# Retention stage: the decode tokens' value rows spread before the outputs, state pairs read between projections, four rows spread at once in the last head

## The chip, the cores and the metric

The kernel runs on one core of one Trainium2 chip. The metric is the device time of one execution in microseconds (us); three executions of the kernel before gave 3306.15, 3307.99 and 3312.09, median 3307.99. The profile is one further execution.

## The reference

The program is one inference step of a 4-layer decoder for 512 prompt tokens and 8 decode tokens that share weights. Layers 0 and 3 use retention as their mixer, layer 1 pooling, layer 2 sparse attention; each is followed by a SwiGLU block and layer norms. The change touches retention only. For a head with keys of 256 and values of 512 the decode part is, for each of the 8 decode tokens b:

```
S_new[b] = gamma * S_old[b] + k[b] (256) outer v[b] (512)      # written back as an output
o[b]     = q[b] @ S_new[b]                                     # 512 values, then normalised and gated
```

For the prompt part, o = (q k^T * decay) v over chunks of 128, and the final state is S = sum over tokens of decayed k outer v. Both parts go through the same weights: y = (silu(g) * normalised o) @ w_out.

## The kernel before

All products with weights are done as three float32r matmuls (high*high, high*low, low*high), in "units" of 128 output columns over 520 tokens (two halves of 260). For a retention layer a head has units 0 to 11 (q, k, v, gate) and 12 to 19 (output projection); unit(i, k) on TensorE waits until the accumulator of two units before is evacuated. ScalarE makes the high part of a weight tile (L445), VectorE the low part (L451): `step(k)` on both engines makes the parts of the unit that is two places on, and it waits for the matmuls of unit k. Accumulators lie in PSUM banks 0 to 3, everything else in banks 4 to 7.

Every engine has its own hand-written order of work; semaphores tie them. Names that the change and the prediction use:

- `outputs(t)` (TensorE, L524 to L526): prompt outputs of chunk t, (t+1) groups of three matmuls of 512 columns. `stats(i, t)` and `centre(i, t)` (VectorE, L1268 to L1277) normalise them, with `rstd` on GpSimd (L614, L616) between.
- `spread_v(i, b)` (TensorE, L1933 and L1934): copies the value row of decode token b to all 128 partitions of bank 7 with two matmuls. It waits until the state of token b-1 is updated (`s_new`), since all rows use one bank.
- `new_state(i, b)` (VectorE, L1300): two instructions that add k[b] times the spread row to the state of token b in place. It waits for `vb` (the spread row) and `st_sc` (state loaded by GpSimd's queue at L608 and scaled by ScalarE at L849).
- `read_states(i, g)` (TensorE, L1943): eight matmuls that read the states of tokens 2g and 2g+1; it waits for their updates. `state_out` and `refill` (GpSimd, L620 and L608) write a state out and load a later one into its buffer; there are four buffers for eight tokens.
- `final_state(d)` (TensorE, L524 to L526), `turn_outputs` (TensorE, L1813 and, for the decode rows, L1914), `gate` and `gate_lo` (VectorE, L1285 and L1291), `gain(n)` (VectorE, L1258).

Heads follow one another: `tail(n)` does the decode work of tokens 4 to 7 of head i-1 between the units of head i. The last head (i = RH - 1 = 3) has no next head, so it does that work by itself before its output projection.

Of the kernel before, what the change touches and what calls it, by code (L numbers as in the profile page):

```python
# [25 lines left out]
SEQ = 512  # L26
NB = 8
T = SEQ + NB
HALF = T // 2
QT = SEQ // P  # L30
# [3 lines left out]
RH, RK, RV = 4, 256, 512  # L34
# [203 lines left out]

VT_BANK, AT_BANK, O_BANK, SF_BANK = [6, 7, 4, 5, 4], [4, 5, 6, 7], [5, 4, 5, 4, 6], [5, 4]
OT_BANK = [5, 4, 5, 4, 7]  # L240


def trunk(nc, A, O):

    with ExitStack() as ctx:
        marks = Marks(nc, ctx)
        S = marks.sem
        V, C, G, M = nc.vector, nc.scalar, nc.gpsimd, nc.tensor
# [22 lines left out]
        ps = ctx.enter_context(nc.psum_tensor("ps", [P, 8, 512], F32))  # L271
# [315 lines left out]
        def _(pool):  # L587
# [4 lines left out]
            def ret(stage):  # L592
                j = int(stage[3:]) // 3
                s_in = A["state_ret"][j].rearrange("b h (d p) e -> h b p d e", p=P)
                s_out = O[3][j].rearrange("b h (d p) e -> h b p d e", p=P)

                def head(ap, i, b=None):
                    return ap[i] if b is None else ap[i, b]

                def head_constants(i):  # L600
                    pool.dma_start(mask, head(A["decay"], i)).then_inc(S["head_in"], 16)
                    pool.dma_start(hc(i, 0, 8), head(A["head_col"], i)).then_inc(S["head_in"], 16)
                    gains = A["ret_norm_g"][j].rearrange("(h c p) -> h p c", p=P, c=VC)
                    with nc.allow_non_contiguous_dma("columns of gains"):
                        pool.dma_start(hc(i, 8, 12), head(gains, i)).then_inc(S["head_in"], 16)

                def state_in(i, b):
                    pool.dma_start(st[:, b % 4], head(s_in, i, b)).then_inc(S[f"st_in{b % 4}"], 16)  # L608

                def rstd(at, t):  # L610

                    n = P if t < QT else 36
                    pool.wait_ge(*at("o_ag", t + 1))
                    G.tensor_scalar(ve[0:n, t:t + 1], mv[0:n, t, 1:2], EPS, None, ALU.add).then_inc(S["rs_e"], 1)  # L614
                    pool.wait_ge(*at("rs_e", t + 1))
                    G.tensor_tensor(rs[0:n, t:t + 1], ve[0:n, t:t + 1], mhalf[0:n, :], ALU.pow).then_inc(S["rs_p"], 1)  # L616

                def state_out(at, i, b):
                    pool.wait_ge(*at("s_new", 2 * b + 2))
                    pool.dma_start(head(s_out, i, b), st[:, b % 4]).then_inc(S[f"st_out{b % 4}"], 16)  # L620

                head_constants(0)
                for b in range(4):
                    state_in(0, b)
                for i in range(RH):
                    at = marks.here(stage, i)

                    def refill(b):

                        pool.wait_ge(*at(f"st_out{b % 4}", 16 * (1 + b // 4)))  # L630
                        pool.wait_ge(*at("so_mm", b // 2 + 1))
                        if b < 4:
                            state_in(i, b + 4)
                        elif i < RH - 1:
                            state_in(i + 1, b - 4)

                    rstd(at, 0)
                    rstd(at, 1)
                    state_out(at, i, 0)
                    state_out(at, i, 1)  # L640
                    rstd(at, 2)
                    rstd(at, 3)
                    state_out(at, i, 2)
                    state_out(at, i, 3)
                    refill(0)
                    refill(1)
                    pool.wait_ge(*at("sf_cp", 2))
                    pool.dma_start(head(O[2][j, 0].rearrange("h (d p) e -> h p d e", p=P), i), sf).then_inc(S["sf_out"], 16)
                    if i < RH - 1:
                        pool.wait_ge(*at("att_m", 4))  # L650
                        head_constants(i + 1)
                    refill(2)
                    refill(3)
                    for b in range(4, 8):
                        state_out(at, i, b)
                    rstd(at, 4)
                    for b in range(4, 8):
                        refill(b)
# [501 lines left out]
        def _(dve):  # L1160
# [35 lines left out]
            def ret(stage):  # L1196
# [3 lines left out]
                def before_gates(i):  # L1200
# [55 lines left out]
                    def gain(n):  # L1256
                        dve.wait_ge(*at("sil_g", n + 1))
                        V.tensor_scalar(sg[:, n], sg[:, n], hc(i, 8 + n, 9 + n), None, ALU.mult  # L1258
                                        ).then_inc(S["sg_n"], 1)
# [34 lines left out]
                    def new_state(i, b):  # L1294

                        at = marks.here(stage, i)
                        dve.wait_ge(*at("vb", b + 1))
                        dve.wait_ge(*at("st_sc", b + 1))
                        for d in range(KC):
                            V.scalar_tensor_tensor(st[:, b % 4, d], ps[:, 7, :], k_f[:, d, SEQ + b:SEQ + b + 1],  # L1300
                                                   st[:, b % 4, d], ALU.mult, ALU.add).then_inc(S["s_new"], 1)

                    def step(k):
# [68 lines left out]
                    gain(0)  # L1372
                    step(9)
                    gain(1)
                    stats(i, 0)
                    stats(i, 1)
                    new_state(i, 0)
                    centre(i, 0)
                    centre(i, 1)
                    step(10)  # L1380
                    gain(2)
                    new_state(i, 1)
                    stats(i, 2)
                    stats(i, 3)
                    centre(i, 2)
                    centre(i, 3)
                    new_state(i, 2)
                    step(11)
                    gain(3)
                    new_state(i, 3)  # L1390
                    gate(i, 0)
                    gate(i, 1)
                    gate_lo(i, 0)
# [417 lines left out]
        def _(pe):  # L1811
# [14 lines left out]
            def ret(stage):  # L1826
# [31 lines left out]
                for i in range(RH):  # L1858
# [67 lines left out]
                    def spread_v(i, b):  # L1926

                        at = marks.here(stage, i)
                        pe.wait_ge(*at("v_lo", 5))
                        if b:  # L1930
                            pe.wait_ge(*at("s_new", 2 * b))
                        one = ident_r[0:NB, b:b + 1].to_broadcast([NB, P])
                        M.matmul(ps[:, 7, :], one, v_h[0:NB, QT, :], start=True, stop=False)  # L1933
                        M.matmul(ps[:, 7, :], one, v_l[0:NB, QT, :], start=False, stop=True).then_inc(S["vb"], 1)  # L1934

                    def read_states(i, g):

# [10 lines left out]
                    def tail(n):  # L1948

                        if not i:  # L1950
                            return
                        h = i - 1
                        if n == 0:
                            turn_outputs(h, 2, ("gate_m", 1))
                            turn_outputs(h, 3, ("gate_m", 2))
                            spread_v(h, 4)
                        elif n == 1:
                            read_states(h, 1)
                            spread_v(h, 5)
                        elif n == 2:  # L1960
                            read_states(h, 2)
                            spread_v(h, 6)
                        elif n == 3:
                            spread_v(h, 7)
                        elif n == 4:
                            read_states(h, 3)
# [28 lines left out]
                    values(3, ("att_m", 2))  # L1995
                    values(4, ("v_lo", 3))
                    unit(i, 9)
                    outputs(0, ("v_lo", 4))
                    outputs(1, ("v_lo", 5))
                    spread_v(i, 0)  # L2000
                    unit(i, 10)
                    spread_v(i, 1)
                    outputs(2, ("o_n", 1))
                    outputs(3, ("o_n", 2))
                    spread_v(i, 2)
                    unit(i, 11)
                    spread_v(i, 3)
                    final_state(0, ("o_n", 3))
                    final_state(1, ("o_n", 4))
                    read_states(i, 0)  # L2010
                    turn_outputs(i, 0, ("sf_cp", 1))
                    turn_outputs(i, 1, ("sf_cp", 2))
                    if i == RH - 1:
                        read_states(i, 1)
                        turn_outputs(i, 2, ("gate_m", 1))
                        turn_outputs(i, 3, ("gate_m", 2))
                        for b in range(4, 8):
                            spread_v(i, b)
                            if b % 2:
                                read_states(i, b // 2)  # L2020
                        turn_outputs(i, 4, ("s_new", 2 * NB))
                        project(i)

# [269 lines left out]
            for stage, n, units in STAGES:  # L2293
# [25 lines left out]
                elif kind == "end":  # L2319
                    at = marks.here(stage)  # L2320
# [65 lines left out]
```

## Time and profile before

| what | value |
|---|---|
| median of three executions | 3307.99 us |
| profiled execution, its own time | 3312.6 us |
| its span, first to last instruction | 3310.9 us |
| mean granted TensorE clock | 0.951 |
| TensorE matmul busy | 3082.7 us (93%) |
| VectorE busy | 1567.0 us (47%) |
| ScalarE busy | 1016.1 us (31%) |
| GpSimd busy | 223.9 us (7%) |

The two retention layers lie in the first fifth of the span and behind its 2330th us. A head repeats every 128.72 us (second spread of a head at 101.83, 230.54, 359.26 us). The granted clock is given as a share: 1.00 is 2.4 GHz and 0.50 is 1.2 GHz.

### The profile page before, as it was taken

To read this page: it belongs to the slowest core of one execution; us is meant where nothing else is said; L and a number is where in the kernel's file an instruction comes from. 1 tells how busy PE (TensorE), PEld (TensorE's weight loads), DVE (VectorE), ACT (ScalarE), POOL (GpSimd) and SP (SyncE) were. 2 spreads that over 40 slices of the span, in tenths; PEclk is the share of its full clock that TensorE was granted. 3 is DMA by queue.
4 is the path that set the end of the run, shared out by engine and by line. 5 is a ranking of instruction groups with operands and counts; after the bars stand their busy time and mean duration, and the time that the engine had idled before them with its cause. 6 is when DMAs were issued, how large, how long until landed. Compare 5 with 4: busy or idle time off the path is not lost.

```text
span 3310.9 us, 54894 instructions
## 1 busy us (share of the span) xinstructions
PE 3082.7 (93%) x23315; PEld 2901.3 (88%) x23315; DVE 1567.0 (47%) x2418; ACT 1016.1 (31%) x1428; POOL 223.9 (7%) x350
## 2 busy tenths in 40 slices
PE   8999997999976999988787899999999999799997
PEld 7898895999975999987677799999889989599996
DVE  4555555333357333358765453234555555533234
ACT  3333332322233222232333142222523333332223
POOL 0111111000000000010001100000021011100000
PEclk9999997999987999999888899999899999799998
DMA  6345333232311332321122323233244433333230
GB/s 146 131 132 159 128 115 124 81 111 71 103 50 54 92 99 83 102 65 44 52 58 71 121 71 103 82 89 96 87 149 125 148 131 115 109 89 108 76 101 35
DMA packets 491331, 323.11 MB, mean 98 GB/s; under 512 B 29179, under 2 KB 467707, under 8 KB 491130
## 3 DMA queue, kind: packets, MB, share of 16 engines
q1 hardware_dynamic: 464338, 230.14, 24.4%
q0 software_dynamic: 26800, 90.18, 8.0%
q8 instruction: 148, 2.42, 0.3%
q14 instruction: 45, 0.37, 0.0%
HBM read 275.90 MB, written 44.82 MB: 97 GB/s over the span
## 4 chain that ended last, share of the span: by engine, by line
PE 75%; issue 14%; DVE 8%; ACT 2%; POOL 0%; DMA 0%; another core or an unknown queue 0%; POOLq 0%; SPq 0%; ACTq 0%; DVEq 0%
PE ps L474 59%; PE ps L1813 2%; PE ps L524 2%; PE ps L1943 2%; PE ps L526 2%; PE ps L525 2%; PE ps L505 1%; PE ps L1933 1%; DVE wf L1533 1%; DVE tiny L1531 1%; DVE wf L1778 1%; PE ps L2276 1%; DVE x_l L1165 1%; PE ps L2288 1%; DVE w_l L451 1%
## 5 line engine op out<-in xcount | busy, mean ns | idle before, releaser
L474 PE MATMUL ps<-x_h,w_h 128*128 128x260 f32 x4576 | 941.6, 287 | 10.4 <-DVE w_l L451 8.2
L474 PE MATMUL ps<-x_h,w_l 128*128 128x260 f32 x4576 | 927.9, 285 | 0.0
L474 PE MATMUL ps<-x_l,w_h 128*128 128x260 f32 x4576 | 926.9, 284 | 0.0
L451 DVE TENSOR_TENSOR w_l<-w_raw,w_h 128x1024 fp32r<-128x1024 f32 (+3 forms) x440 | 528.1, 1200 | 793.9 <-ACT w_h L445 793.2
L474 PEld LDWEIGHTS ps<-x_h,w_h 128*128 128x128 f32 x4576 | 715.4, 191 | 34.2 <-issue 23.7
L445 ACT ACTIVATE w_h<-w_raw 128x1024 fp32r<-128x1024 f32 (+3 forms) x440 | 456.0, 1036 | 904.1 <-PE ps L474 874.3
L474 PEld LDWEIGHTS ps<-x_h,w_l 128*128 128x128 f32 x4576 | 711.6, 190 | 0.0
L474 PEld LDWEIGHTS ps<-x_l,w_h 128*128 128x128 f32 x4576 | 711.4, 190 | 0.0
L474 PE MATMUL ps<-rr,w_h 128*128 128x260 f32 x3968 | 639.3, 283 | 2.2 <-DVE w_l L451 1.1
L474 PEld LDWEIGHTS ps<-rr,w_h 128*128 128x128 f32 x3968 | 543.4, 188 | 4.1 <-issue 3.0
L474 PE MATMUL ps<-rr,w_l 128*128 128x260 f32 x1984 | 399.3, 283 | 0.0
L474 PEld LDWEIGHTS ps<-rr,w_l 128*128 128x128 f32 x1984 | 306.8, 189 | 0.0
L1729 DVE TENSOR_TENSOR wf<-ps,wf 128x520 f32<-128x520 f32 x88 | 61.6, 700 | 248.4 <-PE ps L474 248.4
L1096 ACT ACTIVATE wf<-ps 128x520 f32<-128x520 f32 x88 | 53.2, 605 | 354.9 <-PE ps L474 350.3
L524 PE MATMUL ps<-rr 128*128 128x512 f32 (+5 forms) x332 | 122.8, 373 | 18.2 <-DVE rr L1629 10.4
L751 POOL TENSOR_TENSOR tiny<-tiny 128x5 f32<-128x5 f32 x8 | 14.2, 1772 | 1757.7 <-DVE tiny L1762 1757.7
L1813 PE MATMUL ps<-ident,wf 128*128 128x128 f32 (+4 forms) x607 | 95.2, 291 | 32.3 <-DMA wf<-in_x_sample 9.6
L1743 DVE SCALAR_TENSOR_TENSOR x<-x,ps 128x520 f32<-128x520 f32 x40 | 27.9, 696 | 196.1 <-PE ps L474 196.1
L1813 PEld LDWEIGHTS ps<-ident,wf 128*128 128x128 f32 (+4 forms) x607 | 70.5, 142 | 55.5 <-issue 30.6
L525 PE MATMUL ps<-rr 128*128 128x512 f32 (+5 forms) x332 | 117.4, 355 | 0.0
L526 PE MATMUL ps<-rr 128*128 128x512 f32 (+5 forms) x332 | 117.3, 355 | 0.0
L1300 DVE SCALAR_TENSOR_TENSOR wf<-ps,wf 128x512 f32<-128x512 f32 x128 | 89.8, 744 | 16.5 <-PE ps L1934 13.0
(268 smaller groups left out, 2785.1 us busy)
## 6 DMA issues: line engine op xcount, KB each, us to landing
w_raw<-in_ffn_w_in SPq DMA_DIRECT2D x176, 512.0 KB, 3.9
w_raw<-in_ret_w_in SPq DMA_DIRECT2D x96, 512.0 KB, 4.0
out<-wf POOLq DMA_DIRECT2D x72, 512.0 KB, 3.3
wf<-in_state_ret POOLq DMA_DIRECT2D x64, 512.0 KB, 5.5
w_raw<-in_ffn_w_out SPq DMA_DIRECT2D x32, 768.0 KB, 4.9
w_raw<-in_ffn_w_out SPq DMA_DIRECT2D x32, 640.0 KB, 4.3
w_raw<-in_ret_w_out SPq DMA_DIRECT2D x64, 256.0 KB, 2.9
w_raw<-in_dsa_w_in SPq DMA_DIRECT2D x27, 512.0 KB, 3.9
```

Source lines behind the costliest of these rows:

```text
L445: C.activation(whole(stage, k, w_h[:, n % 2, 0:m]), landed(stage, k, n, m), ACT.Copy).then_inc(S["w_hi"], 1)
L451: V.tensor_tensor(whole(stage, k, w_l[:, n % 2, 0:m]), landed(stage, k, n, m), whole(stage, k, w_h[:, n % 2, 0:m].bitcast(F32)), ALU.subtr ...
L474: mm = M.matmul(ps[:, 2 * (n % 2) + b, 0:HALF], lhs[:, c, :], rhs[:, c, cols], start=(c == 0 and term == 0), stop=(c == cs - 1 and term == 2))
L505: mm = M.matmul(ps[:, 2 * n + b, 0:HALF], lhs, rhs[:, c, cols], start=(c == 0 and term == 0), stop=(c == DC - 1 and term == 2))
L524: M.matmul(out, lhs_h, rhs_h, start=start, stop=False)
L525: M.matmul(out, lhs_h, rhs_l, start=False, stop=False)
L526: return M.matmul(out, lhs_l, rhs_h, start=False, stop=stop)
L1096: C.activation(halves(sil[:, q]), acc[0], ACT.Silu).then_inc(S["sil"], 1)
L1300: V.scalar_tensor_tensor(st[:, b % 4, d], ps[:, 7, :], k_f[:, d, SEQ + b:SEQ + b + 1], st[:, b % 4, d], ALU.mult, ALU.add).then_inc(S["s_n ...
L1729: V.tensor_tensor(halves(h_raw[:, q]), acc[1], halves(sil[:, q]), ALU.mult).then_inc(S["h_raw"], 1)
L1813: return M.transpose(out, src, ident[0:n, 0:n])
L1943: mm = M.matmul(ps[32 * j:32 * j + 4, 6, :], qz[:, i % 2, d, g, j, :], st[:, (2 * g + j) % 4, d, :], start=(g + d == 0), stop=(g == NB // ...
```

## The change

On TensorE, `spread_v(i, 0)` comes before `outputs(0)` and `spread_v(i, 1)` between `outputs(0)` and `outputs(1)`; `spread_v(i, 2)` and the first `read_states` come ahead of `outputs(2)`, `spread_v(i, 3)` ahead of `outputs(3)`; `read_states(i, 1)` comes straight after unit 11. In the last head rows 4 to 7 are spread right after that, into the four accumulator banks. VectorE and GpSimd take the updates and the writes in the matching order.

```
+def spread_bank(i, b):
+    return b - 4 if i == RH - 1 and b >= 4 else 7
# GpSimd
+                    state_out(at, i, 0)
                     rstd(at, 0)
+                    state_out(at, i, 1)
                     rstd(at, 1)
-                    state_out(at, i, 0)
-                    state_out(at, i, 1)
+                    state_out(at, i, 2)
                     rstd(at, 2)
-                    rstd(at, 3)
-                    state_out(at, i, 2)
-                    state_out(at, i, 3)
                     refill(0)
                     refill(1)
+                    state_out(at, i, 3)
+                    rstd(at, 3)
                     pool.wait_ge(*at("sf_cp", 2))
# VectorE (new_state reads ps[:, spread_bank(i, b), :] instead of ps[:, 7, :])
                     step(9)
                     gain(1)
+                    new_state(i, 0)
                     stats(i, 0)
+                    new_state(i, 1)
                     stats(i, 1)
-                    new_state(i, 0)
                     centre(i, 0)
                     centre(i, 1)
                     step(10)
                     gain(2)
-                    new_state(i, 1)
+                    new_state(i, 2)
                     stats(i, 2)
+                    new_state(i, 3)
                     stats(i, 3)
                     centre(i, 2)
                     centre(i, 3)
-                    new_state(i, 2)
                     step(11)
                     gain(3)
-                    new_state(i, 3)
# TensorE, spread_v (both matmuls write ps[:, spread_bank(i, b), :])
                         pe.wait_ge(*at("v_lo", 5))
-                        if b:
+                        if spread_bank(i, b) == 7 and b:
                             pe.wait_ge(*at("s_new", 2 * b))
+                        elif spread_bank(i, b) < 4:
+                            pe.wait_ge(*at("sil_g", 4))
# TensorE, tail(1) of the next head
-                            read_states(h, 1)
                             spread_v(h, 5)
# TensorE, head
                     unit(i, 9)
-                    outputs(0, ("v_lo", 4))
+                    spread_v(i, 0)
+                    outputs(0, ("v_lo", 5))
+                    spread_v(i, 1)
                     outputs(1, ("v_lo", 5))
-                    spread_v(i, 0)
                     unit(i, 10)
-                    spread_v(i, 1)
+                    spread_v(i, 2)
+                    read_states(i, 0)
                     outputs(2, ("o_n", 1))
+                    spread_v(i, 3)
                     outputs(3, ("o_n", 2))
-                    spread_v(i, 2)
                     unit(i, 11)
-                    spread_v(i, 3)
+                    read_states(i, 1)
+                    if i == RH - 1:
+                        for b in range(4, 8):
+                            spread_v(i, b)
                     final_state(0, ("o_n", 3))
                     final_state(1, ("o_n", 4))
-                    read_states(i, 0)
                     turn_outputs(i, 0, ("sf_cp", 1))
                     turn_outputs(i, 1, ("sf_cp", 2))
                     if i == RH - 1:
-                        read_states(i, 1)
                         turn_outputs(i, 2, ("gate_m", 1))
                         turn_outputs(i, 3, ("gate_m", 2))
-                        for b in range(4, 8):
-                            spread_v(i, b)
-                            if b % 2:
-                                read_states(i, b // 2)
+                        read_states(i, 2)
+                        read_states(i, 3)
                         turn_outputs(i, 4, ("s_new", 2 * NB))
                         project(i)
```

## Rows read from the trace of the kernel before

**Rows 1.** The page: busy shares of all engines, and the chain by engine.

```profile
PE 3082.7 (93%) x23315; PEld 2901.3 (88%) x23315; DVE 1567.0 (47%) x2418; ACT 1016.1 (31%) x1428; POOL 223.9 (7%) x350
PE 75%; issue 14%; DVE 8%; ACT 2%; POOL 0%; DMA 0%; another core or an unknown queue 0%; POOLq 0%; SPq 0%; ACTq 0%; DVEq 0%
```

**Rows 2.** Windows: stretch, length, busy per engine, clock, DMA; third head, last head's end.

```profile
281.40:389.00 107.60, 107.60 (x797) 98.03 (x797) 54.70 (x83) 33.87 (x51) 14.63 (x25) 1.00 0.42 133
499.50:545.00 45.50, 34.50 (x163) 21.25 (x163) 17.64 (x30) 11.22 (x16) 8.04 (x12) 0.77 0.39 138
```

**Rows 3.** Timeline of TensorE, first head: start, length, instruction [idle before].

```profile
93.06 0.39 PE L524 MATMUL ps<-rr 128*128 128x512 f32 x1
93.30 0.40 PE L525 MATMUL ps<-rr 128*128 128x512 f32 x1
...
94.89 0.39 PE L526 MATMUL ps<-rr 128*128 128x512 f32 x1
95.21 0.49 PE L1933 MATMUL ps<-rr,ident_r 8*128 8x512 f32 x1
95.55 0.38 PE L1934 MATMUL ps<-rr,ident_r 8*128 8x512 f32 x1
95.86 0.51 PE L474 MATMUL ps<-x_h,w_h 128*128 128x260 f32 x2
...
101.83 0.50 PE L1933 MATMUL ps<-rr,ident_r 8*128 8x512 f32 x1
...
120.52 1.89 PE L1943 MATMUL ps<-wf,tiny 128*4 128x512 f32 x8
```

**Rows 4.** Timeline of ScalarE, first head, after unit 9.

```profile
93.27 0.60 ACT L822 ACTIVATE wf<-ps 128x520 f32<-128x520 f32 x1 [3.09 <-PE ps L474]
93.77 1.05 ACT L445 ACTIVATE w_h<-w_raw 128x1024 fp32r<-128x1024 f32 x1
```

**Rows 5.** Timeline of VectorE, first head, after units 9 and 10.

```profile
94.85 1.22 DVE L451 TENSOR_TENSOR w_l<-w_raw,w_h 128x1024 fp32r<-128x1024 f32 x1 [3.82 <-ACT w_h L445]
95.99 0.48 DVE L1258 TENSOR_SCALAR wf<-wf,headc 128x520 f32<-128x520 f32 x1
96.39 0.69 DVE L1268 BATCH_NORM_STATS2 tiny<-ps 128x6 f32<-128x512 f32 x1
...
98.01 1.39 DVE L1300 SCALAR_TENSOR_TENSOR wf<-ps,wf 128x512 f32<-128x512 f32 x2
...
105.06 1.40 DVE L1300 SCALAR_TENSOR_TENSOR wf<-ps,wf 128x512 f32<-128x512 f32 x2
```

**Rows 6.** The same place in the eighth head: timeline of all engines.

```profile
2789.09 0.39 PE L524 MATMUL ps<-rr 128*128 128x512 f32 x1
...
2792.02 0.48 DVE L1258 TENSOR_SCALAR wf<-wf,headc 128x520 f32<-128x520 f32 x1
```

**Rows 7.** Timeline of the last head of the first retention layer, all engines.

```profile
508.50 1.09 PE L1813 MATMUL ps<-ident,wf 128*128 128x128 f32 x8
...
511.98 1.44 POOL L608 DMA_DIRECT2D wf<-in_state_ret  x2 [0.63 <-PE ps L1943]
...
515.12 1.41 DVE L1300 SCALAR_TENSOR_TENSOR wf<-ps,wf 128x512 f32<-128x512 f32 x2 [0.41 <-ACT wf L849]
...
516.68 0.76 PE L1933 MATMUL ps<-rr,ident_r 8*128 8x512 f32 x1 [3.60 <-DVE wf L1300]
...
519.30 2.43 ACT L849 ACTIVATE wf<-wf,headc 128x1024 f32<-128x1024 f32 x2 [3.19 <-DMA wf<-in_state_ret]
...
525.61 1.41 DVE L1300 SCALAR_TENSOR_TENSOR wf<-ps,wf 128x512 f32<-128x512 f32 x2 [0.87 <-PE ps L1934]
527.08 3.58 PE L1943 MATMUL ps<-wf,tiny 128*4 128x512 f32 x8 [1.50 <-DVE wf L1300]
```

**Rows 8.** Windows around two waits of TensorE; its clock stands before the last two numbers.

```profile
512.00:523.00 11.00, 5.90 (x18) 1.65 (x16) 5.40 (x8) 5.65 (x6) 2.88 (x4) 0.69 0.83 313
1463.50:1466.80 3.30, 0.02 (x1) 0.00 (x0) 2.68 (x5) 1.17 (x3) 1.48 (x4) 1.00 0.68 188
1466.80:1471.20 4.40, 4.39 (x20) 4.21 (x21) 3.52 (x6) 1.16 (x2) 1.97 (x5) 0.61 0.27 68
```

More of the change, by code:

```diff
@@ L1299, in new_state @@
                         for d in range(KC):
-                            V.scalar_tensor_tensor(st[:, b % 4, d], ps[:, 7, :], k_f[:, d, SEQ + b:SEQ + b + 1],
+                            V.scalar_tensor_tensor(st[:, b % 4, d], ps[:, spread_bank(i, b), :], k_f[:, d, SEQ + b:SEQ + b + 1],
                                                    st[:, b % 4, d], ALU.mult, ALU.add).then_inc(S["s_new"], 1)
@@ L1929, in spread_v @@
                         pe.wait_ge(*at("v_lo", 5))
-                        if b:
+                        if spread_bank(i, b) == 7 and b:
                             pe.wait_ge(*at("s_new", 2 * b))
+                        elif spread_bank(i, b) < 4:
+                            pe.wait_ge(*at("sil_g", 4))
                         one = ident_r[0:NB, b:b + 1].to_broadcast([NB, P])
-                        M.matmul(ps[:, 7, :], one, v_h[0:NB, QT, :], start=True, stop=False)
-                        M.matmul(ps[:, 7, :], one, v_l[0:NB, QT, :], start=False, stop=True).then_inc(S["vb"], 1)
+                        M.matmul(ps[:, spread_bank(i, b), :], one, v_h[0:NB, QT, :], start=True, stop=False)
+                        M.matmul(ps[:, spread_bank(i, b), :], one, v_l[0:NB, QT, :], start=False, stop=True).then_inc(S["vb"], 1)
                     def read_states(i, g):
```

## The prediction

> **What bounds the kernel now.** I read the page first, then its chain, then windows over the retention layers, then timelines of single heads. The page shows TensorE busy for 93% of the span while VectorE has 47%, and three quarters of the chain that ended last is TensorE [rows 1]. The reader is to see in the windows that inside a retention layer there are two kinds of stretch. From 281.40 to 389.00 us (units, outputs and tail of a middle head) TensorE is busy for all 107.60 us at clock 1.00: no wait for VectorE, ScalarE or a state load is on the path there. From 499.50 to 545.00 us, the end of the last head, it is busy for 34.50 of 45.50 us and the clock averages 0.77 [rows 2]. So the question for this change has two halves: what can be saved in the two last heads (one in each retention layer), and whether the heads, which are without a gap where no last head ends, stay so. I look at the wait that comes last at each moved instruction.
>
> **Part 1: spread_v(i, 1) between outputs(0) and outputs(1), all eight heads.** Both spreads write bank 7, so the second waits for the first update of a state, `s_new` 2, now directly after outputs(0). On VectorE this update, new_state(i, 0), stands behind step(9) and gain(1), before and after the change. step(9) needs the high part of unit 11's weights, which ScalarE makes only when unit 9 is finished. The rows give this chain in the first head. ScalarE evacuates unit 9 from 93.27 and makes the high part from 93.77, until 94.82 [rows 4]. VectorE has been idle for 3.82 us when it starts the low part at 94.85, then gain(1) runs from 95.99 and the next instruction starts at 96.39 [rows 5]. In the changed kernel that next instruction is new_state(i, 0), which takes 1.39 us as a pair, so it ends at 97.78. From the end of such a pair to the next spread TensorE needs 0.15 us (515.12 + 1.41 = 516.53, spread at 516.68 [rows 7]), so the second spread starts at 97.93.
>
> When is TensorE there? Its first matmul after unit 9 starts at 93.06. Matmuls of 512 columns start 0.23 us apart. A spread costs 0.74 us: from 94.89 + 0.23 = 95.12 to the start of unit 10 at 95.86 [rows 3]. spread(0) and the three matmuls of outputs(0) are therefore done at 93.06 + 0.74 + 0.69 = 94.49. The wait is 97.93 - 94.49 = 3.44 us. Before, this spread stood behind unit 10, some 6 us of matmuls that hid the whole chain (95.86 to 101.83, rows 3); that cover is gone. The outputs, unit 10 and everything behind it are queued behind the waiting spread on TensorE, and nothing later is idle that could take it up, since the middle heads have no gap. The eighth head has the same distance: its first output matmul at 2789.09 and gain(1) at 2792.02, 2.93 us apart, as 93.06 and 95.99 are [rows 3, 5, 6]. So 8 x 3.44 = 27.5 us. Bounds: if new_state(i, 0) were already done when TensorE comes, nothing; if the chain slipped by the other update and statistics that VectorE might have to take first (0.69 + 1.4), 5.5 us a head. The order is fixed by the code and the durations hold in the rows to 0.02 us, so I keep 3.44.
>
> **Part 2: spread 2, reads and spread 3 around outputs(2).** After unit 10 the chain is the same: spread 2 could start at 101.83 in the old time, the update after step(10) and gain(2) runs 105.06 to 106.46, 4.63 us later, plus 0.15 [rows 3, 5]. TensorE has spread 2 (0.74), read_states(0) (1.89 at 120.52, rows 3) and the nine matmuls of outputs(2) (9 x 0.23 = 2.07), in all 4.70, before spread 3. A wait of 0.08 us, which vanishes where the clock is low. I take 0.4 us for all heads; bounds 0 and 2 us.
> VectorE's other moved work (both statistics behind updates) lies beside unit 10 and unit 11, each about 6 us. GpSimd now writes state 0 before rstd(0): one issue of about 0.8 us, hidden by the same units. refill(0) and refill(1) come ahead of rstd(3), again under unit 11. The work itself is the same in number, spreads and reads have both neighbours of other kinds before and after, so moving them costs nothing by itself. SP's queue is not passed by anything.
>
> **Part 3: the clock after these waits.** In this trace a wait of 3.60 us (516.68, rows 7) lies in a stretch of 11.00 us with clock 0.69, which is 0.31 x 11.00 / 0.5 = 6.8 us at the lower level. The idle 3.30 us from 1463.50 are followed by 4.40 us at 0.61, with TensorE busy for 4.39 of them: 0.39 x 4.40 = 1.7 us lost [rows 8]. My wait of 3.4 us lies between dense matmuls, like the second. The price per head is between 0 (no fall) and 3.4 (half of 6.8, all of it filled with matmuls); I take 2.0, close to the 1.7 of the row that it resembles and a little over it, because a fall may begin inside the wait and the lower level then be kept while TensorE starts again. 8 x 2.0 = 16 us.
> The Trainium skill (page "TensorE: Matmul & The Clock Gate", section "HAM oscillation — how this bites in real kernels") speaks against this change: a kernel whose loop waits each time pays the re-throttling in every turn of the loop, and its example has about 1.67 us throttled in each, of which half is lost. By that figure, an estimate, the eight heads lose 8 x 0.83 = 7 us and the sum would be 9 us lower than mine; the trace's own row shows twice that loss for one wait, and I go by the trace.
>
> **Part 4: the two last heads.** Count from the start of the first turn_outputs, T = 508.50. Before, the update of state 4 starts at T + 6.6 (515.12), and the updates of 4 to 7 are strung out by spreads and loads until T + 18.5 (525.61 + 1.41 = 527.02); the last read ends at 527.08 + 3.58, T + 22.2 [rows 7]. After the change the four rows lie ready, so the updates 4 and 5 end at T + 9.3. State 6 needs its load. It is issued after the final state has been copied and written out, about T + 1.6 instead of T + 3.5 (511.98), and the old one was scaled from 519.30, 7.3 us after its issue [rows 7]. So state 6 is scaled from T + 8.9 at the latest, 1.14 us for one, and updates 6 and 7 end at T + 12.8. read_states(2) waits for update 5, starts at T + 9.3 and takes 3.58 us at the lower clock, as now; read_states(3) follows until T + 16.5. That is 5.7 us before the old end. Against it, read_states(1) (1.9 us, which lay under VectorE's gates) and the four spreads (eight matmuls 0.23 us apart and 0.3 at the ends, 2.2 us, which lay in the waits) now stand ahead of T: 4.1 us. Net -1.6, and up to -2.4 where the load lands a microsecond earlier; I take -2.0 for each, -4 us in all. Bounds: the load keeps its old place and nothing is saved from the updates (+4.1 each, +8), or the moved work costs nothing (-5.7 each, -11).
>
> **Sum.** 27.5 + 0.4 + 16 - 4 = 39.9 us. The profiled execution took 3312.6 us (span 3310.9 and 1.7 around it), so it would take 3352.5. It lies 4.6 us over the median of the runs, 3308.0, from which I forecast 3348.
>
> **Rivals.**
> B, the clock hardly falls: the lower level falls largely on the wait itself, or does not come. For it: the wait is shorter than the 3.60 us row, and in the rows from 1463.50 the waiting stretch itself still has clock 1.00. Against: that same wait of 3.30 us was followed by the fall. Price per head 0 to 0.85 (half of the 1.7): 3308 + 24 = 3332 up to 3339. In a sentence of its own: the figure of the clock-gate page of the Trainium skill lies at the upper end of this case.
> C, the clock costs its most: 6.8 us at the lower level behind every wait, full of matmuls, 3.4 each: 3308 + 23.9 + 27.2 = 3359. For it: the fall behind the 3.60 us wait was that long. Against: there TensorE went on having waits, here it has dense units.
> D, the other side: VectorE has the first update done before TensorE asks, so no head waits, and the last heads' saving remains: 3308 - 4 = 3304, down to 3297 if the moved work costs nothing. It decides if the wait per head is under 0.5 us (4 / 8). For it: VectorE is busy 47% only and was idle 3.82 us just there. Against: that idleness ended by ScalarE's high part, behind which the update stands in order; the queue's spare time lies on the wrong side of that wait.
> That the four spreads do not bring their gain, because the loads of states 6 and 7 decide, is the upper bound of part 4; it makes 3360 with my other terms and shares C's place.
>
> **How the numbers follow.** Forecast 68%, own range 3341 to 3356; B 15%; C (with the last remark) 12%; D 5%. The range 3329 to 3361 takes in the forecast, B but for its lowest and most of C; D and the far ends stay out. A measurement of this kernel can tell about 0.2%, 6.6 us, from no change. Forecast, B and C are all slower by more; of D 3% is faster by more than that and 2% lies within it.
>
> **What would show it.** In the profile after: an idle of 3.2 to 3.5 us before the second spread of each head, ended by VectorE L1300, eight times; the first update starting right behind gain(1), 3.3 us after TensorE's first spread; a head repeating every 134 us instead of 128.72; half-clock stretches in the middle heads that had 1.00 throughout; in the last heads four spreads in a row and updates 4 to 7 spanning 6 us instead of 12. Wrong would be: second spreads without a wait (part 1 falls), the waits with the clock at 1.00 throughout (B), or a last head that is shorter by more than 5 us (part 4).

## The result and the profile after

Four executions of the changed kernel took 3347.39 to 3355.47 us, median 3351.04; the kernel before, with one more run beside them, 3307.34. The ratio is 1.0122, 95% interval 1.011 to 1.0134: 1.2% slower, 43.7 us by the medians. The forecast was 3348, range 3329 to 3361. The profiled execution took 3347.39 us, the fastest of the four, with a span of 3345.7 us. Of all executions told below one is left out of its ratio, since it ran in a slow state: 5003.67 us at a mean clock of 0.554, in the kernel with the four spreads behind the turns.

The page of the changed kernel, busy shares and the chain by engine. TensorE's busy time grew by 18 us only. Its share of the chain rose from 75% to 85%, but the share of "issue" (time in which an engine waited for nothing that the profile shows) fell from 14% to 2%, so the two shares say little about the loss.

```profile
PE 3100.5 (93%) x23315; PEld 2915.9 (87%) x23315; DVE 1569.0 (47%) x2418; ACT 1016.0 (30%) x1428; POOL 224.8 (7%) x350
PE 85%; DVE 9%; ACT 3%; issue 2%; POOL 0%; DMA 0%; SPq 0%; ACTq 0%; DVEq 0%; POOLq 0%
```

TensorE's waits over the whole span (who waited, for whom; us in total, times, longest). The first line is the second spread of each head, eight times 3.2 us. The second is the reads of the last heads, one wait of 6.4 us in each layer. The third does not stand in the list of the kernel before: turn_outputs waits for ScalarE's copy of the final state, once in each head.

```profile
PE ps L1940 <- DVE wf L1305: 25.2, 8, 3.2
...
PE ps L1950 <- DVE wf L1305: 12.8, 2, 6.4
...
PE ps L1818 <- ACT wf L865: 2.7, 8, 0.3
```

The timeline of the first head, all engines, answers to [rows 3 to 5]. The update (L1305) starts behind gain (L1263) at 95.17, TensorE has finished outputs(0) (L531) and stands idle for 3.15 us until the update has ended. Then the same spread takes 0.57 us to its second matmul instead of 0.34, and outputs(1) goes on at the lower clock.

```profile
91.94 0.50 PE L1940 MATMUL ps<-rr,ident_r 8*128 8x512 f32 x1
...
93.17 0.40 PE L531 MATMUL ps<-rr 128*128 128x512 f32 x1
...
93.63 1.23 DVE L456 TENSOR_TENSOR w_l<-w_raw,w_h 128x1024 fp32r<-128x1024 f32 x1 [3.81 <-ACT w_h L450]
94.77 0.48 DVE L1263 TENSOR_SCALAR wf<-wf,headc 128x520 f32<-128x520 f32 x1
...
95.17 1.41 DVE L1305 SCALAR_TENSOR_TENSOR wf<-ps,wf 128x512 f32<-128x512 f32 x2
...
96.72 0.76 PE L1940 MATMUL ps<-rr,ident_r 8*128 8x512 f32 x1 [3.15 <-DVE wf L1305]
...
97.29 0.62 PE L1941 MATMUL ps<-rr,ident_r 8*128 8x512 f32 x1
```

Two windows of the changed kernel: the stretch around this wait, at clock 0.78 (0.22 x 15.50 / 0.5 = 6.8 us at the lower level), and a whole middle head, where the kernel before had 1.00 and no idle time [rows 2].

```profile
91.90:107.40 15.50, 12.35 (x62) 10.15 (x61) 7.55 (x12) 2.58 (x3) 3.16 (x6) 0.78 0.29 103
227.20:361.30 134.10, 130.60 (x948) 116.39 (x946) 69.88 (x104) 43.35 (x62) 18.38 (x30) 0.99 0.42 132
```

The length of a head is read from one instruction that comes once in each: ScalarE's silu of unit 9, just after that unit. Kernel before, ScalarE's timeline: 128.71 us between two heads.

```profile
221.99 0.60 ACT L822 ACTIVATE wf<-ps 128x520 f32<-128x520 f32 x1 [3.10 <-PE ps L474]
...
350.70 0.60 ACT L822 ACTIVATE wf<-ps 128x520 f32<-128x520 f32 x1 [3.10 <-PE ps L474]
```

The same of the changed kernel: 134.08 us. The six middle heads, read so, last 134.08 to 135.61 us, together 37.3 us more than before.

```profile
227.38 0.60 ACT L827 ACTIVATE wf<-ps 128x520 f32<-128x520 f32 x1 [3.10 <-PE ps L479]
...
361.46 0.60 ACT L827 ACTIVATE wf<-ps 128x520 f32<-128x520 f32 x1 [3.10 <-PE ps L479]
```

The last head, timeline of the changed kernel, answers to [rows 7]. The first turn is at T = 536.33. From 541.78 the four loaded states are scaled without a break, the eight update instructions run without a break until T + 12.0 (before T + 18.5), both reads end at T + 15.2 (before T + 22.2). In the second layer they end at T + 14.9 (before T + 22.6).

```profile
536.33 0.60 PE L1818 MATMUL ps<-ident,wf 128*128 128x128 f32 x4
...
537.27 1.16 PE L1818 MATMUL ps<-ident,wf 128*128 128x128 f32 x8 [0.34 <-ACT wf L865]
...
538.21 1.44 POOL L613 DMA_DIRECT2D wf<-in_state_ret  x2
...
541.78 4.25 ACT L854 ACTIVATE wf<-wf,headc 128x1024 f32<-128x1024 f32 x4
543.01 5.36 DVE L1305 SCALAR_TENSOR_TENSOR wf<-ps,wf 128x512 f32<-128x512 f32 x8 [0.41 <-ACT wf L854]
...
545.79 5.71 PE L1950 MATMUL ps<-wf,tiny 128*4 128x512 f32 x16 [6.40 <-DVE wf L1305]
```

From the silu of unit 9 of the last head to the sums behind the layer it is 86.98 and 88.18 us in the two layers, before 86.20 and 86.86, though each now holds the same wait as the other heads. The rows of the first layer, kernel before and changed kernel:

```profile
479.42 0.60 ACT L822 ACTIVATE wf<-ps 128x520 f32<-128x520 f32 x1 [3.10 <-PE ps L474]
565.62 0.61 PE L2276 MATMUL ps<-avg,wf 128*128 128x1 f32 x4 [3.45 <-DVE wf L1191]
```

```profile
496.92 0.60 ACT L827 ACTIVATE wf<-ps 128x520 f32<-128x520 f32 x1 [3.10 <-PE ps L479]
583.90 1.40 PE L2283 MATMUL ps<-avg,wf 128*128 128x1 f32 x7 [3.46 <-DVE wf L1196]
```

So the profiled span grew by 37.3 + 2.1 us in the retention layers; the other stages together were 4.6 us shorter in this one execution, which makes the 34.8 us of the spans.

### The profile page after: what moved, and what is told of

Read it like the earlier page. It is cut to its first block, busy times and chain, and to the rows that moved or that the text cites. A ratio compares the mean times of both kernels' runs of the same rounds, so it can differ in the third digit from the quotient of the medians.

```text
span 3345.7 us, 54894 instructions
## 1 busy us (share of the span) xinstructions
PE 3100.5 (93%) x23315; PEld 2915.9 (87%) x23315; DVE 1569.0 (47%) x2418; ACT 1016.0 (30%) x1428; POOL 224.8 (7%) x350
## 4 chain that ended last, share of the span: by engine, by line
PE 85%; DVE 9%; ACT 3%; issue 2%; POOL 0%; DMA 0%; SPq 0%; ACTq 0%; DVEq 0%; POOLq 0%
PE ps L479 70%; PE ps L529 2%; PE ps L1818 2%; PE ps L531 2%; PE ps L530 2%; PE ps L1950 2%; PE ps L510 1%; DVE wf L1783 1%; PE ps L2283 1%; DVE wf L1538 1%; ACT w_h L450 1%; DVE x_l L1170 1%; PE ps L1940 1%; DVE tiny L1536 1%; DVE wf L1773 1%
## 5 line engine op out<-in xcount | busy, mean ns | idle before, releaser
L479 PE MATMUL ps<-x_h,w_h 128*128 128x260 f32 x4576 | 943.1, 288 | 10.4 <-DVE w_l L456 8.2
L529 PE MATMUL ps<-rr 128*128 128x512 f32 (+5 forms) x332 | 129.8, 395 | 18.2 <-DVE rr L1634 10.4
L531 PE MATMUL ps<-rr 128*128 128x512 f32 (+5 forms) x332 | 121.8, 370 | 0.0
L530 PE MATMUL ps<-rr 128*128 128x512 f32 (+5 forms) x332 | 121.3, 368 | 0.0
L529 PEld LDWEIGHTS ps<-rr 128*128 128x128 f32 (+1 forms) x332 | 67.5, 204 | 51.8 <-issue 36.4
```

Of the source, the lines that this page charges most:

```text
L479: mm = M.matmul(ps[:, 2 * (n % 2) + b, 0:HALF], lhs[:, c, :], rhs[:, c, cols], start=(c == 0 and term == 0), stop=(c == cs - 1 and term == 2))
L529: M.matmul(out, lhs_h, rhs_h, start=start, stop=False)
L530: M.matmul(out, lhs_h, rhs_l, start=False, stop=False)
L531: return M.matmul(out, lhs_l, rhs_h, start=False, stop=stop)
```

## The experiments

Each experiment stands beside new runs of the kernel before, and its ratio is to them: their median was 3310.40 us for the first four experiments and 3310.92 for the last four. The traces are one execution of each kernel.

**Row 1 in another bank (e1_row1_bank6).** Nothing is moved; only the buffer for which the second spread waits is replaced by a free one.

```
-    return b - 4 if i == RH - 1 and b >= 4 else 7
+    return b - 4 if i == RH - 1 and b >= 4 else 6 if b == 1 else 7
```

> The changed kernel, but the value row of token 1 is spread into bank 6 instead of bank 7, so its spread need not wait for the update of state 0; all else keeps its place. Theory (the wait and the clock that falls behind it carry the loss): the 3.15 us idle before the second spread is gone in all eight heads and the middle heads keep clock 1.00; 8 x (3.3 + 2.4) = 45 us less than the changed kernel, about 3306 us (3302 to 3310). Rival 1 (the clock falls because small matmuls now stand among the dense ones, with or without a wait): only the waits go, 8 x 3.3 = 26 us less, about 3325. Rival 2 (the loss is in the moved reads and updates themselves): no more than 5 us less, above 3345.

Measured: 3306.94 us, ratio to before 0.999 (0.9981 to 0.9999). The whole loss is gone, and with it both rivals: the small matmuls stand where they stood, and the middle heads keep the full clock. ScalarE's timeline of this kernel gives a head of 129.37 us, and its window over a whole middle head the full clock:

```profile
222.02 0.60 ACT L827 ACTIVATE wf<-ps 128x520 f32<-128x520 f32 x1 [3.10 <-PE ps L479]
...
351.39 0.60 ACT L827 ACTIVATE wf<-ps 128x520 f32<-128x520 f32 x1 [3.10 <-PE ps L479]
```

```profile
221.90:351.30 129.40, 129.06 (x948) 115.20 (x947) 69.70 (x104) 43.36 (x62) 18.39 (x30) 1.00 0.43 137
```

A head is still 0.65 us longer than before; that is taken up below. The last heads of this kernel take 82.05 and 84.99 us from the silu of unit 9 to the sums, 4.15 and 1.87 us less than before, with no wait for a spread in them. This is the cleanest measure of what the rest of the change brings there.

**The update ahead of the weights (e2_update_first).** The shared bank stays, VectorE's order changes.

```
+                    new_state(i, 0)
                     step(9)
                     gain(1)
-                    new_state(i, 0)
                     stats(i, 0)
```

> The changed kernel, but VectorE takes the update of state 0 ahead of step(9) and gain(1); spreads keep their places and bank 7. Theory (the update is late because it stands behind the weights of unit 11): the update starts some 1.7 us earlier or more, right behind the first spread, and ends 2.8 us earlier; the wait shrinks from 3.2 to about 0.5 us in each head, the clock no longer falls; 8 x (2.7 + 2.4) = 41 us less, about 3310 us (3306 to 3316), and 4 us more than with bank 6. Rival (what counts is that two spreads share a bank at all, the place in VectorE's order does not): no change, above 3345.

Measured: 3316.77 us, ratio 1.0022 (1.0013 to 1.0031). The timeline of its first head shows the update right behind the first spread (L1940, 91.99) and a wait of 0.70 us:

```profile
92.76 1.41 DVE L1305 SCALAR_TENSOR_TENSOR wf<-ps,wf 128x512 f32<-128x512 f32 x2 [2.91 <-PE ps L1941]
...
94.31 0.46 PE L1940 MATMUL ps<-rr,ident_r 8*128 8x512 f32 x1 [0.70 <-DVE wf L1305]
```

The rival falls: the place in VectorE's order carries most of the wait, 3.15 us of which 0.70 are left. The size was a little off: 3316.77 us lies just above the expected range, 10 us above the first experiment instead of 4. The median stands between two groups: six executions took 3313.2 to 3316.8 us, five 3319.6 to 3321.5; the trace is of the fastest one, and what the slower five did otherwise is not known. A head is 130.12 us, 0.76 more than there, 6 us for eight; in two of the eight heads (131.62 and 131.66 us to the next) the clock fell as well, 1.5 us each.

**Part 1 alone, in the kernel before (e3_part1_alone).**

```
# VectorE
                     gain(1)
+                    new_state(i, 0)
                     stats(i, 0)
                     stats(i, 1)
-                    new_state(i, 0)
# TensorE
+                    spread_v(i, 0)
+                    outputs(0, ("v_lo", 5))
+                    spread_v(i, 1)
-                    outputs(0, ("v_lo", 4))
                     outputs(1, ("v_lo", 5))
-                    spread_v(i, 0)
                     unit(i, 10)
-                    spread_v(i, 1)
```

> The kernel before, with one thing changed: spread 0 ahead of outputs(0), spread 1 between outputs(0) and outputs(1), and the update of state 0 directly behind gain(1). Theory: this alone brings the wait of 3.2 us and the fall of the clock in all eight heads, 8 x (3.3 + 2.4) = 45 us more than before, about 3352 us (3346 to 3357). Rival (the rest of the change brings a good part of the loss, and the last heads save no more than the 2 us each that were forecast): under 3345.

Measured: 3352.55 us, ratio 1.0129 (1.0113 to 1.0144), 42 us more than before and as slow as the full change. It has neither the moved reads nor the four rows at once, so the loss does not need them. Waits of this kernel: 35.7 us before its spreads, of which 10.4 stood there already in the two last heads; the rest is 8 x 3.2.

```profile
PE ps L1933 <- DVE wf L1300: 35.7, 12, 3.6
```

Its middle heads last 133.4 to 135.0 us; the difference of up to 1.5 us between them goes with the clock, at the lower level for 3.4 us in some and for 6.8 us in others.

**Four rows at once alone, in the kernel before (e4_four_rows_alone).** Banks as in the change, spreads at their old place.

```
                         for b in range(4, 8):
                             spread_v(i, b)
-                            if b % 2:
-                                read_states(i, b // 2)
+                        read_states(i, 2)
+                        read_states(i, 3)
```

> The kernel before, with one thing changed: in the last head rows 4 to 7 are spread into banks 0 to 3 one behind the other, at the place where they stood (behind the turns of chunks 2 and 3), and both reads follow. Theory (the four spreads fit beside VectorE's gates, and the loads of states 6 and 7, still issued behind the second pair of reads, then end the updates): updates end about 15 us behind the first turn instead of 18.5 and 19.0, 3.5 to 4 us saved in each retention layer, 7 to 8 in all: about 3300 us. Rival (the loads decide throughout and the reads at the lower clock take back the rest): 0 to 3 us saved, 3304 to 3307.

Measured: 3301.36 us, ratio 0.9969 (0.9957 to 0.9981), some 9 to 10 us less: a little over the expectation of 7 to 8. Middle heads last 128.72 us as before; the two last heads are 4.3 and 6.0 us shorter. In its last head ScalarE waits for two loads, and VectorE's updates have gaps, ending 15.0 us behind the first turn (14.3 in the second layer):

```profile
516.80 1.15 ACT L854 ACTIVATE wf<-wf,headc 128x1024 f32<-128x1024 f32 x1 [2.26 <-DMA wf<-in_state_ret]
...
519.06 2.43 ACT L854 ACTIVATE wf<-wf,headc 128x1024 f32<-128x1024 f32 x2 [1.11 <-DMA wf<-in_state_ret]
```

**A read behind the final state (e5_read_behind_final).** The remaining 0.65 us of a middle head.

```
-                    read_states(i, 1)
                     if i == RH - 1:
+                        read_states(i, 1)
                         for b in range(4, 8):
                             spread_v(i, b)
                     final_state(0, ("o_n", 3))
                     final_state(1, ("o_n", 4))
+                    if i < RH - 1:
+                        read_states(i, 1)
```

> Row 1 in bank 6 as in the first experiment, and read_states(1) of the first three heads of a layer moved from ahead of final_state(0) to behind final_state(1). The changed kernel's turns wait 0.34 us for ScalarE's copy of the final state, since no read stands between them any more. Theory: this exposed copy is the 0.64 us by which a head of the first experiment is longer than before (129.36 against 128.72); with the read between, a middle head takes 128.8 us or less, the turn waits for nothing, and 6 x 0.5 = 3 us are saved against the first experiment, some 3304 us. Rival (the 0.64 us are the cost of other places of the small matmuls): the head stays at 129.3.

Measured: 3306.17 us, ratio 0.9982 (0.9972 to 0.9991). The intervals overlap that of the first experiment, so the time alone decides little (about 3 us less were expected); the heads do: 128.73 us between these two, 128.73 to 128.79 in all six.

```profile
221.71 0.60 ACT L827 ACTIVATE wf<-ps 128x520 f32<-128x520 f32 x1 [3.10 <-PE ps L479]
...
350.44 0.60 ACT L827 ACTIVATE wf<-ps 128x520 f32<-128x520 f32 x1 [3.10 <-PE ps L479]
```

Its waits show the copy of the final state in the two last heads only, where the read was not moved:

```profile
PE ps L1818 <- ACT wf L865: 0.7, 2, 0.3
```

The wait itself is 0.34 us, half of the 0.65; that the other half belongs to the same gap is argued from both going together, not shown by itself.

**Updates ahead of the gates, last head (e6_updates_ahead_of_gates).** Built on the kernel just told.

```
# VectorE, last head: ahead of the gates instead of behind them
                     gain(3)
+                        new_state(i, 4) ... new_state(i, 7)
                     gate(i, 0)
...
+                        stats(i, 4)          # ahead of gate(i, 2)
+                        centre(i, 4)         # behind gate(i, 3)
# ScalarE, last head
+                        scale_state(i, 4); scale_state(i, 5)
                     sf_copy(0)
+                        scale_state(i, 6); scale_state(i, 7)
                     sf_copy(1)
# GpSimd, last head: refill(2), refill(3) ahead of the write of the final state
# TensorE, last head
                     final_state(0, ("o_n", 3))
+                        read_states(i, 2)
                     final_state(1, ("o_n", 4))
+                        read_states(i, 3)
```

> The kernel of e5_read_behind_final, and in the last head the updates of states 4 to 7 ahead of all gates: ScalarE scales 4 and 5 ahead of the copies of the final state and 6 and 7 between them, GpSimd loads 6 and 7 ahead of the write of the final state, TensorE reads pair 2 between the two final states and pair 3 behind them, VectorE takes the statistics of the decode rows between the gates. Theory (in the last head the end is set by VectorE's gates and then its updates, 6.7 + 5.4 us behind the first turn, while it waits 8 us for that turn): the updates fall into this idle time, the 6.4 us wait of the reads goes, 7 to 9 us less in each layer than with e5_read_behind_final, about 3288 us. Rival (states 6 and 7 land too late, and the gates now wait behind them): 0 to 4 us less, 3300 or more.

Measured: 3289.77 us, ratio to before 0.9934 (0.992 to 0.9947), 16 us under e5_read_behind_final, as the theory had it. This version beats both kernels, by 21 and by some 60 us. Its timeline in the first layer: two updates under the spreads and final_state(0), two behind their loads, 3.39 us of idle time between, all over before the first turn at 516.74, and the 6.4 us wait is gone. In the second layer one read still waits, for 1.5 us. Several things were moved together here, so the gain is that of the whole arrangement.

```profile
505.84 2.73 DVE L1312 SCALAR_TENSOR_TENSOR wf<-ps,wf 128x512 f32<-128x512 f32 x4 [0.23 <-PE ps L1949]
...
511.95 2.73 DVE L1312 SCALAR_TENSOR_TENSOR wf<-ps,wf 128x512 f32<-128x512 f32 x4 [3.39 <-ACT wf L857]
...
516.74 1.09 PE L1826 MATMUL ps<-ident,wf 128*128 128x128 f32 x8
```

**The four spreads behind the turns (e7_rows_behind_turns).** Based on the first experiment; the loop over rows 4 to 7 stands behind turn_outputs(i, 3) in the last head.

> Row 1 in bank 6 as in the first experiment, and in the last head the four spreads of rows 4 to 7 behind the turns of chunks 2 and 3 instead of right behind unit 11. Forecast's view (four spreads ahead of the first turn cost their full time, 2 us a layer, and are free beside VectorE's gates): the last heads are 1.9 us shorter each, 4 us less than the first experiment, about 3303. Rival (the place of the spreads is free, as the clock behind them differs): within 1 us of the first experiment.

Measured: 3302.75 us without the execution of 5003.67 us (3303.3 with it), ratio 0.9974 (0.9964 to 0.9985), against 0.999 in the first experiment: about 5 us less, where 4 were expected. The traces show where: from the silu of unit 9 to the first turn it is 31.04 us in both layers, against 33.10 in the first layer of the first experiment, 2.06 less. Four spreads in a row take 8 x 0.23 + 0.3 us, as forecast: the first starts at 514.57, the eighth matmul at 516.29.

**Late loads (e8_late_loads).** Based on the first experiment; read_states(1) of the last head stands behind the first two turns.

> Row 1 in bank 6 as in the first experiment, and in the last head read_states(1) behind the first two turns as in the kernel before, so that the loads of states 6 and 7 are issued some 2 us later against the turn. Theory (the early loads are what the forecast missed; they let the four updates run back to back, 5.36 us): now updates 6 and 7 wait for their loads, the updates end 2 to 3 us later behind the first turn, while the read's 1.9 us ahead of it are saved: 0 to +2 us against the first experiment. Rival (loads are never late, the gain comes from the banks alone): 3 to 4 us less than the first experiment.

Measured: 3304.65 us, ratio 0.9982 (0.9973 to 0.9991), about 2.6 us less than the first experiment, with overlapping intervals, where 0 to 2 more were expected and the rival had 3 to 4 less. The expectation failed in its mechanism: the loads of states 6 and 7 are issued at 518.61, 4.0 us behind the first turn (514.62), and yet VectorE's updates run without a break. ScalarE scales the third state 4.3 us behind the issue and waits 0.28 us for it:

```profile
521.73 5.36 DVE L1305 SCALAR_TENSOR_TENSOR wf<-ps,wf 128x512 f32<-128x512 f32 x8 [0.41 <-ACT wf L854]
...
522.94 2.44 ACT L854 ACTIVATE wf<-wf,headc 128x1024 f32<-128x1024 f32 x2 [0.28 <-DMA wf<-in_state_ret]
```

So issuing this pair 2 us later did not delay the updates. In this kernel states 4 and 5 were loaded long before, behind the early read_states(0). In e4_four_rows_alone their loads are issued at the turns, with the write of the final state and the other two loads right behind them, and ScalarE waits for two of them. That this crowding of transfers is the cause is argued, not shown: no run moves the first pair's loads alone.

## Why the prediction was right, point by point

- **Part 1, the wait (27.5 us).** Right. TensorE could have gone on at 93.17 + 0.23 = 93.40 and went on at 96.72: 3.32 us against 3.44. Eight of them make 26.6. With another bank the wait was gone, with VectorE's order changed it fell to 0.70 us; part 1 added alone to the kernel before it brought 42 us.
- **Part 2 (0.4 us).** The spread before outputs(3) waits for nothing that the list of waits shows. What part 2 had wrong is the sentence that moving reads "costs nothing by itself". read_states(0) had stood between final_state(1) and the turns and hidden ScalarE's copy. Without it a head is 0.64 us longer (129.36 against 128.72), 4 us in the six middle heads. With another read put in that place (e5_read_behind_final) the head is back at 128.7. The step that failed was that only the arrival of the moved instruction was looked at, not what its old place covered.
- **Part 3, the clock (16 us).** Right, near its size. Middle heads average 134.93 us; less 129.36 of the first experiment and the wait of 3.3 leaves 2.3 us a head, between the bounds 0 and 3.4. The clock fell in all eight heads, to the lower of its two levels, 1.2 instead of 2.4 GHz. So rival B falls. The price follows the length of the fall: middle heads with 3.4 us at the lower level come out 1.4 us longer than wait and copy explain, those with 6.8 us 2.3 to 2.9. The measured 2.3 is nearer to the 1.7 us of the trace's own row than to the 0.83 us that was estimated from the Trainium skill (page "TensorE: Matmul & The Clock Gate", section "HAM oscillation — how this bites in real kernels"). That page's account of a loop that pays again in every turn agrees with this trace, eight times of eight.
- **Part 4, the last heads (-4 us).** The mechanism was right, the size too small. In the first experiment, which has no wait for a spread, the two last heads are 4.15 and 1.87 us shorter than before, 6 us in all, the copy's 0.6 us each included. The part ahead of the turn held: 33.10 us from the silu of unit 9 to the first turn in its first layer, before 29.07, so 4.0 us against 4.1. The mis-sized term is the chain behind the turn. The forecast had the reads end at T + 16.5, 5.7 us earlier than before; they ended at T + 15.2 and T + 14.9, which is 7.0 and 7.7 us earlier. Both reads start where they were expected, T + 9.5 against T + 9.3. The forecast gave each of them 3.58 us at the lower clock, but only the first ran so: the clock went back to its full level during the second, which took 2.3 us. The loads do not explain it. The last update ended at T + 12.0 and not T + 12.8, but the second read began behind the first, at T + 12.8, and in the last experiment later loads left the row of updates unbroken. Two windows of the changed kernel show the two reads:

```profile
545.79:549.40 3.61, 3.60 (x10) 0.60 (x12) 2.58 (x4) 0.24 (x1) 2.17 (x3) 0.50 0.86 321
549.40:551.60 2.20, 2.10 (x8) 0.21 (x4) 0.04 (x1) 0.00 (x0) 0.00 (x0) 0.85 0.95 357
```

- **A term that the forecast did not have.** The output projection behind the reads also got shorter, by 2.6 us in the first layer and 1.3 in the second, with the same work and the same waits. In the first layer its clock averaged 0.88 before and 1.00 after. How much of this is the change and how much luck is open: where such a fall lands differs from trace to trace, and the last heads of the first experiment and of e5_read_behind_final, which are alike, take 82.05 to 85.06 us. Kernel before and changed kernel:

```profile
530.66:565.60 34.94, 28.08 (x200) 26.96 (x200) 21.11 (x36) 9.62 (x17) 0.79 (x2) 0.88 0.29 84
```

```profile
551.50:583.90 32.40, 25.51 (x202) 24.39 (x201) 21.12 (x36) 9.64 (x17) 0.80 (x2) 1.00 0.33 97
```

- **The sum.** The heads of the two traces differ by 39.4 us. Going through the first experiment they split into 26.6 for the waits, 14.9 for what the clock cost in all eight heads (2.3 in a middle head, less in the last ones, where the first experiment has falls of its own), 3.9 for the copy in six middle heads and -6.0 for the two last ones. The forecast had 27.5, 16, 0.4 and -4. So the two large terms were right, and two small misses, 3.5 us too few and 2 us too few of saving, partly cancelled; that the total of 39.9 comes so close is partly luck. The medians say 43.7, with 4 us between the fastest and the median run of the changed kernel; the profiled execution is the fastest one, and its other stages were 4.6 us shorter.
- **The signs.** One sign named for a failure of part 4, a last head shorter by more than 5 us, is met or not by how one counts. The first experiment shows 4.15 and 1.87. Taking wait, clock and copy of an average middle head (6.2 us) from the changed kernel's own last heads, which are 0.8 and 1.3 us longer than before, gives 5.4 and 4.9, but the clock did not cost that much there.
- **Rival D** fell at its own point of decision: the wait is 3.3 us, not under 0.5. C, too: the lower level lasted 3.4 us in three heads and 6.8 in five, and part of it lay under the wait, as the clock of 0.91 in this window around the first head's wait shows. All of rival B (3332 to 3339) lay inside the range 3329 to 3361, so the range alone could not have told it from the forecast; the granted clock did.

```profile
93.50:96.70 3.20, 0.07 (x1) 0.01 (x1) 3.07 (x5) 1.14 (x2) 0.00 (x0) 0.91 0.15 44
```

## What to carry to other kernels

Before a producer is moved closer to its consumer, follow the order of work of the engine that must free the buffer. Here the update was short and VectorE mostly idle, but the update stood behind an instruction that could not start until the matmuls being left behind were done, and a shared buffer turned that into a wait of the engine that bounds everything. One free buffer for the second row took the whole loss away. Ask also what the moved instruction covered at its old place. And where one engine waits at the end of a loop for a row of instructions of another, look whether that row fits into the other engine's idle time earlier, as the updates ahead of the gates did.

## What the runs showed of the hardware

The clock can fall without any wait. In the last head of the changed kernel TensorE is busy for all of the 9.00 us from 525.00 (reads of 4 columns of weights, then eight spread matmuls of 8 rows, then dense ones), and its clock averages 0.81 there; it had been at the full level for the dense matmuls of unit 11. Windows of the changed kernel, first layer and the same place of the second:

```profile
525.00:534.00 9.00, 9.00 (x34) 5.68 (x33) 1.09 (x2) 1.40 (x3) 0.00 (x0) 0.81 0.10 31
...
2851.00:2861.00 10.00, 10.00 (x48) 6.69 (x47) 1.09 (x2) 1.72 (x3) 0.00 (x0) 1.00 0.11 32
```

It is not so each time: in the second layer the same place ran at the full level. The first experiment shows it the other way round, a fall in the second layer (clock 0.86 from 2812.00 to 2824.00, TensorE busy throughout) and none in the first. In the kernel with the update ahead of the weights a wait of only 0.7 us was followed by a fall in two heads of eight. What decides between a fall and none was not tried.
